# VectorE's order in differential attention, and the router rows' shift added by TensorE products of depth 1

## The reference

```python
def diff_attention(q, k, v, lambda_qk, subln_g, lam_init):
    s = jnp.einsum('bqhsd,bkhsd->bshqk', qblk, k) * scale      # two score maps per head
    p = jax.nn.softmax(s, axis=-1)
    a = p[:, 0] - lam * p[:, 1]                                # the combination
    o = jnp.einsum('bhqk,bkhe->bqhe', a, v)
    ...
conv = gb * short_conv(gc * xin, conv_w)                       # the rest of the mixer

h = rms_norm(x, g_ffn) * (1 + scale2) + shift2                 # layer 1: the router's rows
logits = h @ w_router
top_v, top_i = lax.top_k(logits, TOP_K)
y = sum over the two experts of gate * swiglu_expert(h)
```

## Time and profile before

| | us |
|---|---|
| median of 3 runs | 1950.79 (1949.42 to 1951.01) |
| the profiled execution | 1948.53 |
| its span | 1946.7 |
| TensorE busy | 1887.4 (97%) |
| VectorE busy | 1118.3 (57%) |
| ScalarE busy | 799.6 (41%) |
| GpSimd busy | 139.3 (7%) |

### The profile page before, as it was taken

The page is one execution under the profiler, slowest core; times in us unless marked ns, Lnnn a source line. Parts: engine busy times, 40 slices in busy tenths (PEclk is TensorE's granted clock), DMA queues, the critical chain, the costliest instruction groups (busy, mean ns, idle before and its releaser), DMA issues.

```text
span 1946.7 us, 30525 instructions
## 1 busy us (share of the span) xinstructions
PE 1887.4 (97%) x12501; PEld 1726.0 (89%) x12501; DVE 1118.3 (57%) x1796; ACT 799.6 (41%) x1334; POOL 139.3 (7%) x109
## 2 busy tenths in 40 slices
PE   7999989999999999999998899899999999999998
PEld 6999767999999999999997587889898988989896
DVE  2644776544432444447347853667676766768577
ACT  4221264322211222223213643556565655656564
POOL 2000000200000000110000012220000000002211
PEclk8999999999999999999999999999999999999999
DMA  9425100324231432315271031677677676768762
GB/s 353 162 105 217 55 1 23 109 98 183 77 120 44 168 127 74 119 34 195 92 211 34 1 66 61 149 239 243 224 246 226 214 237 203 248 200 304 255 200 76
DMA packets 94068, 291.55 MB, mean 150 GB/s; under 512 B 15348, under 2 KB 23924, under 8 KB 93920
## 3 DMA queue, kind: packets, MB, share of 16 engines
q1 hardware_dynamic: 86784, 271.20, 42.3%
q0 software_dynamic: 7136, 18.30, 2.9%
HBM read 283.02 MB, written 12.28 MB: 152 GB/s over the span
## 4 chain that ended last, share of the span: by engine, by line
PE 90%; DVE 5%; ACT 1%; DMA 1%; issue 1%; SPq 0%; POOL 0%; POOLq 0%; ACTq 0%; DVEq 0%
PE ps L740 47%; PE ps L1119 12%; PE ps L1108 12%; PE ps L1109 6%; PE ps L806 2%; PE ps L935 2%; PE ps L1112 2%; PE ps L881 1%; DVE pr L2037 1%; DVE nbias L2020 1%; PE ps L1111 1%; PE ps L1204 1%; DMA ada_raw<-ada_w 1%; PE ps L942 1%; ACT pT L1448 0%
## 5 line engine op out<-in xcount | busy, mean ns | idle before, releaser
L1867 DVE TENSOR_TENSOR w_lo<-raw,w_hi 128x1024 fp32r<-128x1024 f32 x394 | 482.1, 1225 | 386.0 <-ACT w_hi L1319 377.4
L1319 ACT ACTIVATE w_hi<-raw 128x1024 fp32r<-128x1024 f32 x394 | 414.5, 1053 | 341.7 <-PE ps L740 171.2
L1108 PE MATMUL ps<-hg,w_hi 128*128 128x416 f32 x1232 | 379.2, 365 | 1.0 <-DVE hg L2311 0.8
L740 PE MATMUL ps<-a_hi,w_hi 128*128 128x320 f32 x1472 | 341.9, 313 | 3.4 <-DVE a_lo L1898 3.4
L740 PE MATMUL ps<-a_hi,w_lo 128*128 128x320 f32 x1472 | 336.7, 310 | 0.0
L740 PE MATMUL ps<-a_lo,w_hi 128*128 128x320 f32 x1472 | 333.8, 308 | 0.0
L1109 PE MATMUL ps<-hg,w_lo 128*128 128x208 f32 x1232 | 319.2, 259 | 0.0
L740 PEld LDWEIGHTS ps<-a_hi,w_hi 128*128 128x128 f32 x1472 | 247.4, 188 | 12.1 <-issue 8.1
L740 PEld LDWEIGHTS ps<-a_lo,w_hi 128*128 128x128 f32 x1472 | 248.6, 189 | 0.0
L740 PEld LDWEIGHTS ps<-a_hi,w_lo 128*128 128x128 f32 x1472 | 245.2, 188 | 0.0
L1109 PEld LDWEIGHTS ps<-hg,w_lo 128*128 128x128 f32 x1232 | 234.7, 191 | 0.4
(11 more groups left out here) (285 smaller groups left out, 2446.5 us busy)
## 6 DMA issues: line engine op xcount, KB each, us to landing
raw<-gu_w SPq DMA_DIRECT2D x220, 512.0 KB, 4.4
raw<-moe_down_w SPq DMA_DIRECT2D x88, 512.0 KB, 4.2
ada_raw<-ada_w SPq DMA_DIRECT2D x21, 2048.0 KB, 8.3
raw<-in_w SPq DMA_DIRECT2D x48, 512.0 KB, 9.8
raw<-down_w SPq DMA_DIRECT2D x22, 512.0 KB, 3.4
raw<-out_w SPq DMA_DIRECT2D x16, 512.0 KB, 3.5
ada_pro<-ada_w SPq DMA_DIRECT2D x2, 2048.0 KB, 19.2
y_rows<-ey POOLq DMA_DIRECT2D x7, 512.0 KB, 3.5
```

What stands on the lines that cost most here:

```text
L740: ins = nc.tensor.matmul(out[:, hf, 0:c1 - c0], w, o[:, c0:c1], start=f, stop=e)
L1108: nc.tensor.matmul(sums, whi, both, start=(k == 0), stop=False)
L1319: nc.scalar.activation(w_hi[:, s, :], raw[:, n % RAW, :], ACT.Copy).then_inc(hi_done, 1)
L1867: nc.vector.tensor_tensor(w_lo[:, s, :], raw[:, n % RAW, :], w_hi[:, s, :].bitcast(F32), ALU.subtract)\
```

## The change

It has two parts.

In attention, VectorE's `combine(i)` comes before `take_output(i - 2)`, and combination 1 with maxima 5 and 6 moves from step 1 into the last block of the input projection, ahead of the mixer's remainder.

In routing, x g + root * shift is formed on TensorE before the scaling: the five columns of the root are transposed to one row (1 x 640) amid the logits, ScalarE copies that row to SBUF in two pieces, and `tile_rows` adds to each tile two products of depth 1 (the root's row for the tile x the shift's row, 2 x 512 columns) in the same PSUM slot. ScalarE scales all five tiles. GpSimd's three additions and VectorE's two tiles go. The shift is loaded to one partition.

```diff
-ROWS_BY_POOL = 3
+        root_row = pr[:].rearrange("p a b c -> p (a b c)")[0:1, 2 * D:2 * D + T]
...
-                        sp.dma_start(shift_rows[:, c, :], shifts_d[c].partition_broadcast(P)).then_inc(shift_in, 16)
+                        sp.dma_start(shift_rows[0:1, c, :], shifts_d[c:c + 1, :]).then_inc(shift_in, 16)
...
-                        if t < ROWS_BY_POOL:
-                            sp.wait_ge(ht_pool, t + 1)
-                        else:
-                            sp.wait_ge(ht_dve, t - ROWS_BY_POOL + 1)
+                        sp.wait_ge(ht_scaled, t + 1)
...
-                    logits_of(2, KB).then_inc(mm_done, 1)
+                    logits_of(2, KB - 3)
+                    ng = NORM_AT[2 * l + 1][2] % 4
+                    pe.wait_ge(root_done, 2)
+                    for t in range(TT):
+                        at = ps[0:1, ng, 1, t * P:(t + 1) * P] if t < 4 else ps[0:1, ng, 0, P:2 * P]
+                        ins = nc.tensor.transpose(at, rms[:, 1, t:t + 1], idn[:])
+                    ins.then_inc(root_turned, 1)
+                    logits_of(KB - 3, KB).then_inc(mm_done, 1)
...
                         for k in range(KB):
-                            ins = nc.tensor.transpose(ps[:, (rg + b) % 4, k // 4, (k % 4) * P:(k % 4 + 1) * P],
-                                                      hraw[:, k, t * P:(t + 1) * P], idn[:])
+                            nc.tensor.matmul(ps[:, (rg + b) % 4, k // 4, (k % 4) * P:(k % 4 + 1) * P],
+                                             hraw[:, k, t * P:(t + 1) * P], idn[:],
+                                             start=k % 4 == 0, stop=False, is_transpose=True)
+                        if t == 0:
+                            pe.wait_ge(shift_in, 32)
+                            pe.wait_ge(row_ready, 1)
+                        for hf in range(2):
+                            ins = nc.tensor.matmul(ps[:, (rg + b) % 4, hf, 0:512], root_row[:, t * P:(t + 1) * P],
+                                                   shift_rows[0:1, min(t, 1), hf * 512:(hf + 1) * 512],
+                                                   start=False, stop=True)
                         ins.then_inc(mm_done, 1)
...
+                    act.wait_ge(root_turned, 1)
+                    nc.scalar.activation(root_row[:, 0:4 * P], ps[0:1, ng, 1, 0:4 * P], ACT.Copy)
+                    nc.scalar.activation(root_row[:, 4 * P:T], ps[0:1, ng, 0, P:2 * P], ACT.Copy).then_inc(row_ready, 1)
...
-                    for b, t in ((1, 0), (3, 1), (4, 2)):
+                    for b, t in ((1, 0), (3, 1), (4, 2), (5, 3), (7, 4)):
...
-            pool.wait_ge(shift_in, 32)
-            for t in range(ROWS_BY_POOL):
-                pool.wait_ge(ht_scaled, t + 1)
-                nc.gpsimd.tensor_tensor(ht[:, t, :], ht[:, t, :], shift_rows[:, min(t, 1), :], ALU.add)\
-                    .then_inc(ht_pool, 1)
...
+                        if last:
+                            combine(1)
+                            row_max(5)
+                            row_max(6)
                         link(with_bias(gcx[:, j, :], tt[:, 1, :], c % 8, cv))
...
                     if i >= 2:
+                        combine(i)
                         take_output(i - 2)
-                    if i:
-                        combine(i)
                         row_max(2 * i + 3)
                         row_max(2 * i + 4)
...
-                    shifted_rows(5, 3)
+                    token_rows(3)
...
-                    shifted_rows(7, 4)
+                    token_rows(4)
```

More of the change, by code:

```diff
@@ L463, in hybrid_step @@
         ht_scaled = sem("ht_scaled")
-        ht_pool = sem("ht_pool")
-        ht_dve = sem("ht_dve")
+        root_turned = sem("root_turned")
+        row_ready = sem("row_ready")
         h_done = sem("h_done")
@@ L1334, in root @@
                 act.wait_ge(mm_done, q0 + 1)
-                nc.scalar.activation(rms[:, 0, :], ps[:, g0 % 4, 0, 0:TT], ACT.Sqrt,
+                nc.scalar.activation(rms[:, 1 if i else 0, :], ps[:, g0 % 4, 0, 0:TT], ACT.Sqrt,
                                      bias=eps[:, 0:1], scale=1.0 / width).then_inc(root_done, 1)
@@ L1632, in main_expert @@
                             elif kind == "xt":
-                                if i == 0:
-                                    act.wait_ge(ht_pool, ROWS_BY_POOL)
-                                    act.wait_ge(ht_dve, TT - ROWS_BY_POOL)
                                 act.wait_ge(mm_done, q0 + q + 1)
@@ L1875, in reciprocal_root @@
                 dve.wait_ge(root_done, 2 if i else 1)
-                link(nc.vector.reciprocal(rms[:, 0, :], rms[:, 0, :]))
+                link(nc.vector.reciprocal(rms[:, 0, :], rms[:, 1 if i else 0, :]))
                 if i == 0:
@@ L1880, in reciprocal_root @@
                     dve.sem_inc(rms_ready, 1)
+                    dve.wait_ge(row_ready, 1)
                     dve.sem_inc(blk_free, 1)
@@ L2240, in token_rows @@
                         dve.sem_inc(blk_free, 1)
-                    def shifted_rows(b, t):
-                        dve.wait_ge(mm_done, rq + b + 1)
-                        if t == ROWS_BY_POOL:
-                            dve.wait_ge(shift_in, 32)
-                        nc.vector.scalar_tensor_tensor(halves(ht[:, t, :]), ps[:, (rg + b) % 4], rms[:, 0, t:t + 1],
-                                                       halves(shift_rows[:, 1, :]), op0=ALU.mult, op1=ALU.add)\
-                            .then_inc(ht_dve, 1)
-                        dve.wait_ge(ht_dve, t - ROWS_BY_POOL + 1)
-                        dve.sem_inc(blk_free, 1)
                     dve.wait_ge(lgT_ready, 1)
```

## The result

| | before | after |
|---|---|---|
| median, us | 1950.15 (4 runs, 1949.42 to 1951.01) | 1961.12 (4 runs, 1959.53 to 1964.38) |
| the profiled execution | 1948.53 | 1959.53 |
| its span | 1946.7 | 1957.7 |

The ratio is 1.0058, with a 95% interval of 1.0045 to 1.007. The kernel became slower by 11 us, where the prediction had 1.4 us faster and a range up to 1953.2.

A forecast was written before the change was run, and what follows sets the result against it. TensorE holds 90% of the chain; VectorE's copy delays attention, and VectorE and GpSimd bound the routing. Attention -3.2 and routing +1.8 give -1.4 us from the median 1950.79: 1949.4 us, own range 1946.1 to 1952.8, wider range 1945.6 to 1953.2.

The forecast's parts named there:

- the routing's sum: Layer 1's routing: slot numbers 2.53 us later, less 0.78, so the first expert 1.8 us later; ends +0.2 to +3.5.
- the clock falls over the routing: Slower rival: TensorE at half clock from last logits to slot numbers, 18.8 us costing as much again, 1968 us; chance 0.09.
- the upper end that it named for a tile: Routing: the added products of depth 1 take 3.4 us a tile at half the clock, where 1.71 was forecast.
- the +3.5: Upper end of the routing's loss in us, with every pass a fifth dearer (20 x 0.09).
- the slack of 0.78: Routing: VectorE's low part of the gathered rows had stood 0.78 us behind its list of places, subtracted from 2.53.
- Steps 3 and 4: Attention, steps 3 and 4 of each five: without the copy ahead of the combination, TensorE's own round remains, saving 0.35 us each.
- Step 5: Attention, a context step with 128 keys: VectorE waits for the copy in both orders, change 0.
- Step 6: Attention: VectorE is the bound; the copy now stands behind the combination and is also waited for, change 0 (+0.01).
- Step 7: Attention: combination and copy end 2.75 us behind the exponential's start, the scores 2.63, a loss of 0.12 us.
- a round: Attention, five steps: 0.70 - 0.13 = 0.57 us gained, three times a layer.
- The start: Start of a layer's attention: combination 1 must wait for exponential 3, turn 2 at 242.68 against 242.24, loss 0.44 us.
- The 3.4 us: Routing: time VectorE's cast and subtraction would lose without GpSimd beside them; changes nothing in the forecast, since TensorE comes later.

## Why the prediction was wrong

*The step that failed* is the granted clock, which the routing's sum took as full from the first tile to the slot numbers; the prediction weighed the opposite only as the rival "the clock falls over the routing", put at 0.09 because "the clock was half only behind the idle 4.83 us". That reading of the earlier trace rows was true of transpositions, and the kernel with nothing but these confirms it: they keep the clock. It was carried over to products of depth 1, of which the trace of before had none. The prediction noticed that for their duration, and bounded it from both sides; for their effect on the clock it gave no bound. Even the upper end that it named for a tile, 3.4 us at half the clock, did not go into the range: the +3.5 there has every pass only a fifth dearer. The runs showed in its place that products over 1 row, in turn with transpositions, let the granted clock fall to 0.50 within two tiles, and over 128 rows keep it at 1.00. The rival's own price was too high: it named 18.8 us that cost as much again, 1968; the stretch to the slot numbers cost 40.56 - 29.71 = 10.85 more, and 1.2 more behind it, because the first tile still ran at the full clock and the last did again.

*The products' cost* was right: 4 passes in 1.72 to 1.82 us, forecast 1.71. The root's transpositions 0.64 (1196.66 to 1197.30), forecast 0.56.

*The sum of the routing at full clock* came out: with 128 rows the first expert comes 47.93 - 45.91 = 2.02 later, forecast 1.8, and the kernel is 2.6 us slower by the median than the one with attention alone. Two errors cancel in the sum, and from one execution to another this distance moves by up to 1.8 us. That the kernel whose clock is kept took 1949.53 us, where 1949.4 was forecast, is luck: the forecast started from a median of 1950.79, and against the 1949.3 of the same rounds this kernel gained nothing (ratio 1.0002, 0.9992 to 1.0011) where 1.4 us had been forecast. The mask's product came 2.62 later counted from the sums, forecast 2.58, but from it to the slot numbers it took 5.14 and not 5.75. So the slot numbers came 1.96 later, not 2.53. And of the slack of 0.78 nothing was got back, for behind them it took 18.22 to the first expert against 18.16. With 128 rows TensorE's turn of the stream waited there for VectorE's queue, which it had not done before, and which the sum did not have. VectorE only passes on there that ScalarE has copied a tile of the stream; those four copies ran from 1226.60 to 1230.37:

```profile
1230.35 1.09 PE L1187 MATMUL ps<-idn,x 128*128 128x128 f32 x8 [3.46 <-DVEq L2457]
```

One number of the routing doesn't add up as it stands: VectorE's chosen rows, 3.1 us behind a mask product at 1215.97, would be there at 1219.07 and not 1219.9. Nothing hangs on it, for both are earlier than 1221.7.

*Attention.* Steps 3 and 4: saved 0.37 and 0.33, forecast 0.35 each. Step 5: 4.00 in both. Step 6: 4.38 (253.10 to 257.48) against 4.29, a loss of 0.09 where 0.01 stood; the copy, which the turn now waits for [0.55 <-DVE ada_raw], costs that. Step 7: 3.63 against 3.48, loss 0.15 for 0.12. So 0.46 a round instead of 0.57. The start: turn 2 comes 7.00 us behind the scores of 234.13, before 6.50; a loss of 0.50 for 0.44. Sum: 0.50 - 3 x 0.46 - 0.35 = -1.23, measured -1.29, forecast -1.62. So the new order's mechanism was right and a layer's gain was put a quarter too high. What the forecast did not have is the fall of the clock at the start of layer 1.

*GpSimd and VectorE.* The 3.4 us were right, and also that they change nothing as long as TensorE comes later.

## What to carry to other kernels

When work is moved onto TensorE, ask of its form whether it keeps the clock, and not only how many passes it takes: here products that use 1 or 32 of the 128 rows let the granted clock fall while the engine was busy all the time, and what stood behind them took double until products over all rows had brought it back. Padding the contraction with zero rows cost no pass and kept the clock. An idle engine is not free room by itself: over 128 rows the new work filled the idle time as forecast (the mask's product came 2.62 us later, forecast 2.58), and over one row the same work cost 12 us more.

For an order of instructions that helps some steps of a round and hurts others, take the steps one by one: the two that gained gave 2.4 us a layer alone and 1.3 with the rest, where the clock did not fall. The medians don't tell the two orders apart.

## What the runs showed of the hardware

- Products over 1 and over 32 rows, in turn with transpositions, TensorE busy 100%: granted clock 0.50 (with 1 row 5.60 us of 5.60 us busy, with 32 rows 5.00 of 5.00, 1211 to 1216). The same over 128 rows, 127 of them zero: 1.00. Zero data did not lower it.
- Transpositions in float32 alone, nearly all of 128 x 128, 11.6 us long: granted clock 1.00.
- The Trainium skill (TensorE: Matmul & The Clock Gate, Part 1: The HAM clock gate) lets the clock follow how busy TensorE has been. By that rule the clock of after would have stayed up; the rows of after have it fall with the engine busy throughout, so busy time as the profile counts it is not all that decides.
- VectorE's cast of 40 numbers a row takes 1.56 us beside GpSimd's additions and 0.18 without them, a subtraction of 5 takes 2.25 and 0.17.
